# A hybrid attention layer on one core: queries, dilated keys and memory keys projected with their features on the partitions, split once, kept in HBM and read back per unit of work

## What is computed

```python
h = jnp.einsum('bsd,de->bse', x, w_in[l]) + b_in[l]
qa, ka, va, qb, kb, vb, qc, z = jnp.split(h, split_idx, axis=-1)
oa, _ = banded_causal_attention(apply_rope(heads(qa, SWA_Q_HEADS), cos, sin),
                                apply_rope(heads(ka, SWA_KV_HEADS), cos, sin),
                                heads(va, SWA_KV_HEADS), SWA_WINDOW - 1, attn_sinks[l])
ob = dilated_attention(apply_rope(heads(qb, DIL_HEADS), cos, sin),
                       apply_rope(heads(kb, DIL_HEADS), cos, sin), heads(vb, DIL_HEADS))
mkv = jnp.einsum('bmd,de->bme', mem, w_mem[l])
mk, mv = jnp.split(mkv, 2, axis=-1)
oc = memory_attention(heads(qc, MEM_HEADS), heads(mk, MEM_HEADS), heads(mv, MEM_HEADS))
y = jnp.concatenate([rms_normalize(oa), rms_normalize(ob), rms_normalize(oc)], axis=-1)
y = y * g_branch[l] * jax.nn.silu(z)
y = jnp.einsum('bse,ed->bsd', y, w_out[l])
x = layer_norm(DEEPNORM_ALPHA * x + y, ln_gain[l], ln_bias[l])
```

## Time and profile before

| | |
|---|---|
| Median of 3 runs | 548.54 us (548.5 to 549.79) |
| Span of the profiled execution, its only time on the page | 548.2 us |
| PE busy | 524.6 us, 96% |
| DVE busy | 341.3 us, 62% |
| ACT busy | 263.0 us, 48% |
| POOL busy | 100.0 us, 18% |
| DMA | 35.35 MB, 64 GB/s on the mean |
| Projections (first chunk and jobs) | until 185.0 us |

### The profile page before, as it was taken

The page is one execution under the profiler, slowest core; times in us unless marked ns, Lnnn a source line. Parts: engine busy times, 40 slices in busy tenths (PEclk is TensorE's granted clock), DMA queues, the critical chain, the costliest instruction groups (busy, mean ns, idle before and its releaser), DMA issues.

```text
span 548.2 us, 10413 instructions
## 1 busy us (share of the span) xinstructions
PE 524.6 (96%) x3728; PEld 480.9 (88%) x3728; DVE 341.3 (62%) x1034; ACT 263.0 (48%) x601; POOL 100.0 (18%) x133
## 2 busy tenths in 40 slices
PE   5989999999999999999999989999999999999993
PEld 5989999999999888888888778889889888989982
DVE  4675643787677545454555677775867566665633
ACT  5432330122100165656566688575757566666530
POOL 0000000000000012211222021242515150431415
PEclk9999999999999999999999989999999999999998
DMA  8960420120200011101110480010100101020021
GB/s 295 384 171 2 145 88 11 68 74 6 78 1 1 1 39 39 38 2 40 39 39 2 154 277 31 2 54 25 68 12 39 39 39 40 2 77 1 2 78 77
DMA packets 15154, 35.35 MB, mean 64 GB/s; under 512 B 3456, under 2 KB 6144, under 8 KB 15104
## 3 DMA queue, kind: packets, MB, share of 16 engines
q1 hardware_dynamic: 14528, 33.64, 17.7%
q10 hardware_dynamic: 576, 1.05, 0.5%
HBM read 30.49 MB, written 4.19 MB: 63 GB/s over the span
## 4 chain that ended last, share of the span: by engine, by line
PE 85%; DVE 6%; SPq 3%; DMA 2%; ACT 2%; issue 1%; POOLq 0%; POOL 0%; DVEq 0%; ACTq 0%
PE long_ps L751 15%; PE o_ps L718 11%; PE wide L581 8%; PE wide L583 8%; PE wide L582 8%; PE narrow L700 7%; PE long_ps L650 4%; PE long_ps L652 4%; PE long_ps L651 4%; PE wide L689 3%; PE wide L688 3%; DMA mem_raw<-in_mem_t 2%; PE narrow L664 2%; SPq L487 1%; PE narrow L728 1%
## 5 line engine op out<-in xcount | busy, mean ns | idle before, releaser
L581 PE MATMUL wide<-w_hi,x_hi 128*128 128x256 f32 x384 | 108.5, 283 | 0.6 <-DVE w_lo L965 0.6
L583 PE MATMUL wide<-w_hi,x_lo 128*128 128x256 f32 x384 | 107.1, 279 | 0.0
L582 PE MATMUL wide<-w_lo,x_hi 128*128 128x256 f32 x384 | 107.1, 279 | 0.0
L879 ACT ACTIVATE prob<-prob,nb 128x256 f32<-128x256 f32 (+7 forms) x96 | 52.9, 582 | 56.9 <-DVE nb L1128 37.4
L1090 DVE SCALAR_TENSOR_TENSOR q_lo<-narrow,q_hi 128x256 fp32r<-128x256 f32 x80 | 29.4, 368 | 73.7 <-ACT q_hi L863 73.7
L1224 POOL COPY q<-qo 128x256 f32<-128x256 f32 x80 | 28.9, 379 | 247.8 <-DVE qo L1047 92.6
L581 PEld LDWEIGHTS wide<-w_hi,x_hi 128*128 128x128 f32 x384 | 72.9, 190 | 0.7 <-issue 0.7
L582 PEld LDWEIGHTS wide<-w_lo,x_hi 128*128 128x128 f32 x384 | 73.2, 190 | 0.0
L583 PEld LDWEIGHTS wide<-w_hi,x_lo 128*128 128x128 f32 x384 | 72.7, 189 | 0.0
L863 ACT ACTIVATE q_hi<-narrow 128x256 fp32r<-128x256 f32 x80 | 26.6, 332 | 69.6 <-DVE neg_sink L1075 39.9
L892 ACT ACTIVATE prob_t<-narrow 128x512 f32<-128x512 f32 (+3 forms) x96 | 49.1, 528 | 19.1 <-PE narrow L700 18.6
(11 more groups left out here) (136 smaller groups left out, 1173.2 us busy)
## 6 DMA issues: line engine op xcount, KB each, us to landing
w_raw<-in_w_qkv SPq DMA_DIRECT2D x12, 512.0 KB, 4.7
x_raw<-in_x_t SPq DMA_DIRECT2D x16, 256.0 KB, 7.9
g_raw<-in_w_gate SPq DMA_DIRECT2D x8, 512.0 KB, 3.3
wo_raw<-in_w_out SPq DMA_DIRECT2D x8, 512.0 KB, 3.7
res<-in_x SPq DMA_DIRECT2D x8, 512.0 KB, 3.5
out<-res SPq DMA_DIRECT2D x7, 512.0 KB, 2.6
w_raw<-in_w_mem SPq DMA_DIRECT2D x4, 512.0 KB, 7.9
mem_raw<-in_mem_t SPq DMA_DIRECT2D x1, 1024.0 KB, 13.1
```

What stands on the lines that cost most here:

```text
L581: pe.matmul(dst, t_hi[:, k, cols], w_hi[s][:, k, :], start=(k == 0), stop=False)
L582: pe.matmul(dst, t_hi[:, k, cols], w_lo[s][:, k, :], start=False, stop=False)
L583: mm = pe.matmul(dst, t_lo[:, k, cols], w_hi[s][:, k, :], start=False, stop=(k == KT - 1))
L879: e = act.activation(prob[s][:, cols], src, ACT.Exp, bias=nb[:, r, hh:hh + 1])
```

## The change

The features of `mk`, `qc`, `kb` and the three `q` chunks are now projected with the features on the partitions: a job is 256 columns of weights with 256 tokens, 48 matmuls of 128x256 with the weights as the stationary side (31 jobs instead of 52, in which `kva` and `mv` are as before). The weight columns of a rotated chunk are put in another order on the host, first halves of the four heads, then second halves, so that rotation is done between two PSUM halves with cosine and sine tables of the same layout (`cos_t`, `sin_t`). DVE does this into `turn` (`finish_turned`), ACT rounds into `spill`, DVE writes the rest beside it (`turned_lo`), and SP stores both to HBM (`store_turned`). Keys are read back in one go (`load_turned_keys`), the queries of a unit into one of four slots, twice, into partitions 0 to 63 and 64 to 127 (`load_queries`). POOL's copies, PE's query transposes and the roundings and splits per unit are gone. The spill buffers lie under the probability buffers, `turn` under `gate_e`, `sin_t` under `mask_b`. SP's queue is written as a loop that follows the units. The bias row holds 512 values instead of 1792.

```diff
+GROUP = 4
+TURNED = ("mk", "qc", "kb", "q")
...
-PREPARED = {3: (4, (5, 6, 6, 7)), 4: (9, (10, 10, 11, 11)), 5: (13, (13, 14, 14, 15)), 6: (16, (17, 17, 18, 18)),
-            7: (29, (30, 31, 32, 33)), 8: (37, (38, 39, 40, 41)), "g0": (44, (45, 46)), "g1": (46, (47, 48))}
-QS = 3
-Q2 = 3
+PREPARED = {3: (4, (5, 6, 6, 7)), 4: (8, (9, 9, 10, 10)), 5: (11, (11, 11, 12, 12)), 6: (13, (13, 13, 14, 14)),
+            7: (18, (18, 19, 19, 20)), 8: (22, (22, 23, 23, 24)), "g0": (26, (27, 27)), "g1": (27, (28, 28))}
+QS = 4
+QUERIES_AT = 28
...
+GATE_LOAD_AT = [4 * f - 4 for f in range(FT)]
+WO_LOAD_AT = [LAST_TILE_AT + k // 2 for k in range(FT)]
...
-        q_hi = [at(f"q_hi{s}", [P, 2 * P], F32R, q_at + s * nbytes(2 * P)) for s in range(QS)]
-        q_lo = [at(f"q_lo{s}", [P, 2 * P], F32R, q_at + (QS + s) * nbytes(2 * P)) for s in range(QS)]
+        spill = [at(f"spill{s}", [P, 2, 2, C], F32R, r_t.base + s * nbytes(SEQ)) for s in range(2)]
+        q_at = r_t.base + nbytes(2 * SEQ)
+        q_pair = [at(f"q_pair{s}", [P, 2, 2 * P], F32R, q_at + s * nbytes(2, 2, P)) for s in range(QS)]
...
-            sp.dma_start(b_row[:, :], b_in[0, 0:QKV].partition_broadcast(P)).then_inc(bias_in, 16)
+            sp.dma_start(b_row[:, 0:C], b_in[0, COL_KA:COL_KA + C].partition_broadcast(P)).then_inc(bias_in, 16)
+            sp.dma_start(b_row[:, C:2 * C], b_in[0, COL_VB:COL_VB + C].partition_broadcast(P)).then_inc(bias_in, 16)
...
+            def store_turned(n):
+                c, i = jobs[n]
+                kind, m = kinds[c][0], plan.turned.index(n)
+                sp.wait_ge(turn_split, m + 1)
+                rows = HD if kind in ("mk", "qc") else HD // 2
+                for half in range(2):
+                    if rows == HD:
+                        where = slice(2 * half, 2 * half + 2), slice(0, HD)
+                    else:
+                        where = slice(0, GROUP), slice(half * rows, (half + 1) * rows)
+                    if kind in ("mk", "kb"):
+                        dst = (mk_spill if kind == "mk" else kb_spill[i])[where]
+                        sp.dma_start(dst, f32(spill[m % 2][:, half, :, :])).then_inc(spilled[m % 2], 16)
+                        continue
+                    for b in range(2):
+                        dst = q_spill[2 * i + b, kinds[c][3]][where]
+                        sp.dma_start(dst, f32(spill[m % 2][:, half, b, :])).then_inc(spilled[m % 2], 16)
+            def load_turned_keys(n):
+                c, i = jobs[n]
+                sp.wait_ge(*spills(n))
+                if kinds[c][0] == "mk":
+                    src, dst = mk_spill, k_c[:, :, :]
+                else:
+                    src, dst = kb_spill[i], k_b[:, :, i * C:(i + 1) * C]
+                for piece in range(2):
+                    sp.dma_start(f32(dst[piece * HD:(piece + 1) * HD]),
+                                 src[:, :, piece * C:(piece + 1) * C].rearrange("h d t -> d h t"))\
+                      .then_inc(turned_keys_in, 16)
...
+            def load_queries(u):
+                i, g, heads = query_heads(u)
+                n = heads.stop - heads.start
+                if u >= QS:
+                    sp.wait_ge(wide_full, scores_turn(u - QS) + 1)
+                sp.wait_ge(*spills(query_job(u)))
+                for half in range(2):
+                    sp.dma_start(f32(q_pair[u % QS][half * HD:(half + 1) * HD, 0:n, :]),
+                                 q_spill[i, g, heads].rearrange("h d t -> d h t"))\
+                      .then_inc(q_in[u % QS], 16)
...
+            for n in range(n_jobs):
+                for c in range(4, len(kinds)):
+                    if plan.last_job[c - 3] == n:
+                        load_chunk(c)
+                if plan.last_job[6] == n:
+                    for f in range(2):
+                        load_gate(f)
+                if n in plan.turned:
+                    store_turned(n)
+                before = n - 2
+                if before in plan.turned and kinds[jobs[before][0]][0] in ("mk", "kb"):
+                    load_turned_keys(before)
+                if n >= QUERIES_AT and n - QUERIES_AT < n_jobs - QUERIES_AT:
+                    load_queries(n - QUERIES_AT)
+            for u in range(n_jobs - QUERIES_AT, QS):
+                load_queries(u)
+            sp.wait_ge(h_read, n_jobs)
+            sp.dma_start(mask_b[:, :], mask_b_d).then_inc(mask_b_in, 16)
...
+            for v in range(ITERATIONS + 3):
+                if QS <= v + QS - 1 < n_units:
+                    load_queries(v + QS - 1)
+                for f in range(2, FT):
+                    if v == GATE_LOAD_AT[f]:
+                        load_gate(f)
+                for k in range(FT):
+                    if v == WO_LOAD_AT[k]:
+                        load_wo(k)
...
+                if kinds[c][0] in TURNED:
+                    cols = slice(i * C, (i + 1) * C)
+                    for half in range(2):
+                        dst, f = bank[:, half * C:(half + 1) * C], slice(half * P, (half + 1) * P)
+                        for k in range(KT):
+                            if half == 0 and k % (KT // 2) == 0:
+                                h = 2 * k // KT
+                                pe.wait_ge(chunk_rounded, 2 * (c - 1) + h + 1)
+                                pe.wait_ge(chunk_split, 4 * (c - 1) + 2 * (h + 1))
+                            pe.matmul(dst, w_hi[s][:, k, f], t_hi[:, k, cols], start=(k == 0), stop=False)
+                            pe.matmul(dst, w_hi[s][:, k, f], t_lo[:, k, cols], start=False, stop=False)
+                            mm = pe.matmul(dst, w_lo[s][:, k, f], t_hi[:, k, cols], start=False, stop=(k == KT - 1))
+                    mm.then_inc(wide_full, 1)
+                    return
...
-            def transpose_q(u):
-                heads = UNITS[u][3]
...
-                t.then_inc(narrow_full, 1)
-
             def score(u):
                 kind, i, h0, heads, nk = UNITS[u]
-                split = plan.narrow["q", u]
-                pe.wait_ge(narrow_read[split % 2], split // 2 + 1)
+                q = q_pair[u % QS]
+                pe.wait_ge(q_in[u % QS], 32 * (u // QS + 1))
                 if u == 0:
                     pe.wait_ge(h_read, n_jobs)
+                    pe.wait_ge(turned_keys_in, 32 * (MEM // C + SEQ // C))
...
-                if v + 1 < n_units:
-                    transpose_q(v + 1)
...
+            def turned_hi(n):
+                c, _ = jobs[n]
+                kind, m = kinds[c][0], plan.turned.index(n)
+                if m >= 2:
+                    act.wait_ge(*spills(plan.turned[m - 2]))
+                if kind in ("mk", "qc"):
+                    act.wait_ge(h_read, n + 1)
+                else:
+                    act.wait_ge(turn_rotated, rotated.index(n) + 1)
+                src = turn[:, 0:2, :]
+                if kind in ("mk", "kb"):
+                    dst = spill[m % 2].rearrange("p a c t -> p c a t")[:, 0]
+                else:
+                    src = src.rearrange("p a (b t) -> p a b t", b=2)
+                    dst = spill[m % 2].rearrange("p a b (c t) -> p c a b t", c=2)[:, 0]
+                act.activation(dst, src, ACT.Copy, scale=1.0 if kind in ("mk", "kb") else SCALE)\
+                   .then_inc(turn_rounded, 1)
...
-            unit_q_hi(0)
+            act.wait_ge(turn_split, len(plan.turned))
+            for n in plan.turned[-2:]:
+                act.wait_ge(*spills(n))
...
+            def finish_turned(n, bank):
+                c, i = jobs[n]
+                m = plan.turned.index(n)
+                if m:
+                    dve.wait_ge(turn_split, m)
+                if kinds[c][0] == "mk":
+                    dve.tensor_copy(turn[:, 0:2, :], bank[:, :].rearrange("p (a t) -> p a t", a=2)).then_inc(h_read, 1)
+                    return
+                if m == 1:
+                    dve.wait_ge(turns_in, 48)
+                b = turn_bias[:, 4 if kinds[c][0] == "kb" else kinds[c][3], :]
+                first, second = bank[:, 0:C], bank[:, C:2 * C]
+                if kinds[c][0] == "qc":
+                    dve.tensor_scalar(turn[:, 0, :], first, b[:, 0:1], None, ALU.add)
+                    dve.tensor_scalar(turn[:, 1, :], second, b[:, 1:2], None, ALU.add)\
+                       .then_inc(h_read, 1)
+                    return
+                cos, sin = cos_t[:, i * C:(i + 1) * C], sin_t[:, i * C:(i + 1) * C]
+                dve.scalar_tensor_tensor(turn[:, 0, :], first, b[:, 0:1], cos, ALU.add, ALU.mult)
+                dve.scalar_tensor_tensor(turn[:, 2, :], second, b[:, 1:2], sin, ALU.add, ALU.mult)\
+                   .then_inc(turn_parts, 1)
+                dve.scalar_tensor_tensor(turn[:, 1, :], second, b[:, 1:2], cos, ALU.add, ALU.mult)
+                dve.scalar_tensor_tensor(turn[:, 3, :], first, b[:, 0:1], sin, ALU.add, ALU.mult).then_inc(h_read, 1)
+                m_rot = rotated.index(n)
```

(17 more changed lines are left out.)

283 lines of the change are left out of this document (139 added, 144 removed).

## The result

The changed kernel takes 551.76 us in the median (550.66 to 553.32), against 548.12 for the kernel before in the same comparison: ratio 1.0067, 95% interval 1.0044 to 1.009. That is slower by 0.7%, where 532.2 was forecast and "slower" had a chance of 0.05. The profiled execution took 550.91 us with a span of 549.0, 17.2 above the forecast's 531.85.

A forecast was written before the change was run, and what follows sets the result against it. TensorE (PE) was taken as the bound, 85% of the chain. Terms -14.1 - 4.6 - 0.6 - 1.4 - 3.25 + 1.9 + 5.4 + 0.3 = -16.35 on a 548.2 us span gave 531.85, median 532.2; range 528 to 539.

The forecast's parts named there:

- the landing in the hand-over: From projections to units: last spill store lands 2.6 us after issue, 8.0 us behind the first gate matmul.
- Rival (a): Stores of 4 heads x 32 rows use 4 of 16 DMA engines; last landing at 11.9 us, total 536; chance 0.3.
- Hand-over: From projections to units: PE stands 3.7 us for the first exponential, plus 1.7 for the lower clock: +5.4 us.
- The queries' way back: Unit loop: query loads from HBM have about 12 us or more and land in under 5, costing 0.
- Projections: Start and projections: -7.6 us; key transposes -4.6, start -3.25, weight wait +0.3, exchanged matmuls costed at nothing.
- The start's term: Wait for first rotated keys: shorter bias row takes off 1.6 us, and the lower clock behind it goes: -3.25 together.
- The loop: Unit loop: -14.2 us; query transposes -14.1, waits at the transposes of y -0.6, other waits -1.4, tight exponentials +1.9.
- gate half: Unit loop: PE's 1.1 us wait for it and a long exponential wait shrink, with the clock: -1.4 us.
- bound iterations: Unit loop: in 14 of 80 pairs of exponential and transposes, removing query transposes buys nothing: +1.9 us.
- (c): Unit loop: scores, maximum and exponential set the pace in half of 80 units: about +5 us, 537; chance 0.13.
- (d): Unit loop: SP's single queue becomes the bound at 2.98 us per issue: +150, about 680 us; chance 0.05.
- The sign set for a time over 540: Whole kernel: such a time would mean queries arrive late or the exchanged projections run at another pitch.

The follow-up runs named there:

- the kernel with side-by-side rows: Changed kernel with query stores cut by head and both blocks of a query row side by side in HBM, four stores per job: 535.39 us, ratio 0.9768.
- the fastest version: Side-by-side rows plus swapped probability buffers, each waited for by its first writer, and the mask loaded ahead of the last stores: 529.65 us, ratio 0.9663.
- the first of them alone: Side-by-side rows plus only the swapped probability buffers, each waited for by its first writer: 537.33 us, ratio 0.9804.
- The same program: Changed kernel with dilated-key and query stores issued one head at a time, profiled twice unchanged: 534.67 and 538.63 us.

## Why the prediction was wrong

**The step that failed** in the forecast's own sum is the landing in the hand-over: "the last lands 2.6 after its issue, as an output block of 512 KB does", 8.0 us behind the first gate matmul. The stores were taken to be as fast as one of 128 rows, and a late landing in earlier jobs was put at nothing. Measured: 7.8 us from the last issue in the late jobs (once 9.9), and a last landing at 23.85. Rival (a) had the mechanism, at its rate (24 GB/s per engine worked out, 24.5 measured, 5.5 us per job against 5.44), but was given 0.3 and a price of 4, and it failed at the step "Inside the projections that is just the length of a job, and two spill buffers absorb it". The four engines were counted as if the stores had them alone. They also carry a share of every load. With 5.44 of 5.65 us taken there is no room for the 2.7 us of a weight chunk or for reading the keys back: what is lost there is won back by 0.2 a job only. At the end of the projections ACT is 9.0 us late (it rounds the last job 11.66 us behind the first gate matmul, in the kernel with side-by-side rows 2.62), and the last job's stores queue behind those of the job before: (a)'s landing at 11.9 us behind the first gate matmul became 23.85. The issues were too cheap as well: 2.0 and 2.4 us each on the chain at 122.5 and 124.9, where 0.35 was taken.

**Hand-over.** Forecast +5.4, measured +20.9 by the table's cut. In the changed kernel PE stands 9.5 and 7.6 us instead of 3.7, 13.4 more, and two stands bring the lower clock twice (192.7 to 197.5 and 205.9 to 210.9, some 2.4 us each) instead of 1.7 once. With the stores spread, it measured as forecast: landing 7.7 (8.0), stand 3.3 (3.7).

**The queries' way back**, "0", was right for the loop (160 loads, median landings of 2.7 and 2.2 us, no wait of PE for them) and wrong for unit 0, whose load stood in SP's queue behind a job's stores. It was no cause of its own: moved forward, it gained nothing.

**Projections.** Forecast -7.6 with the start, measured -4.6. The start's term is right, by the kernel with the bias row at its old length. "The shapes and the pitch of both kinds are what these rows already have" was not: the rows had two pitches, and I had read one. At 0.1178 for 946 matmuls, against 0.1178 for 250 and 0.1133 for the rest before, the difference is some 3.1 us. In executions at the faster pitch it isn't lost: the fastest version's profile has its first gate matmul at 176.81, -8.2.

**The loop.** Forecast -14.2 (transposes, y, gate half, bound iterations), measured -15.1. No query transposes; PE's waits for exponentials beside the first are 3.6 us against 3.4 before, the wait at the transposes of y is 0.2 instead of 0.6, and the wait for a gate half that was to go is still there (1.0 of 1.1). Against the second profile of the kernel before the loop has -13.7, so the terms in it are not told apart one by one. Rivals (c) and (d) did not occur.

**What was not weighed.** The range ended at 539, though the working itself put 5.5 us of stores on a job of 5.44. Such a balance has no bound at one job's delay: here it cost 15.5 us more at the hand-over than forecast, and with twice the stores' time per job, at outer count 2, the kernel took 615. The sign set for a time over 540 (late queries, or another pitch of the projections) came true in both parts, but the first was only the way in which the stores' lateness reached PE, and the second is worth 3.1 us.

## What to carry to other kernels

Look at the outermost dimension of both sides of every DMA that a change adds (here it was the HBM side of the stores): 4 instead of 32 cost 13.5 us, 2 for the queries cost 77, and cutting the same bytes by another dimension took it back. A producer and its stores that need the same time per turn are not balanced but on the edge, since every other load also passes through the few engines in use. When a wait at a hand-over goes, ask for the next condition of the same instruction and of the next unit: two edits shortened the hand-over by 4.8 us together, and the first of them alone was worth nothing (the second alone was not run).

## What the runs showed of the hardware

- Stores of 1 KB rows ran at 49 GB/s with an outer count of 2 and at 98 with 4, at busy shares of 0.14 and 0.28: 24.5 GB/s per engine, if 2 and 4 of the 16 carry them. Stores that read 32 partitions landed in 1.7 us (64 KB) and 2.2 us (128 KB), in the same kernel those of 128 KB from 128 partitions in 1.8: 0.4 us apart.
- A ring of two spill buffers whose stores take 5.44 of a job's 5.65 us lost 2.3 us at 1 MB of gate weights loaded beside it and won 0.2 us back per job.
- A stream of 128x256 matmuls runs at one of two pitches, 0.1133 or 0.1178 us, with a granted clock of 1.00 in both. It kept it for up to 946 matmuls; changes were seen at matmuls of another kind (at 99.7 us in the kernel before, at 73.5 and 90.2 in the one with transposes between the jobs), and at four of that kernel's six groups nothing changed. The same program had either (534.67 and 538.63 us). What decides it stays open. It moved the end of the projections by 4.3 us between two profiles of one program, more than half of what one per cent of this kernel is.
